# Decode attention: reading a whole segment's page numbers ahead of its first load

## The reference

```
past_kv = cache_kv_latent[l][page_table].reshape(DB, past_len, KV_LORA)
past_pe = cache_k_rope[l][page_table].reshape(DB, past_len, QK_ROPE)
o_lat = mla_attend(q_lat, q_pe, ((past_kv, past_pe, past_mask), (c_kv, k_pe, self_mask)))
```

## Time and profile before

| what | value |
|---|---|
| time, median of 3 runs | 1570.84 us (1568.0, 1570.84, 1571.12) |
| the profiled execution's own time | 1564.77 us |
| its span | 1563.0 us |
| PE busy | 1468.2 us, 94% of the span |
| PE busy in the slices of the decode attention | 7 to 8 tenths |
| granted TensorE clock, mean | 0.975 of full speed |
| page loads | 128 of 128 KB and 128 of 32 KB, from SP and POOL |

### The profile page before, as it was taken

The page is one execution under the profiler, slowest core; times in us unless marked ns, Lnnn a source line. Parts: engine busy times, 40 slices in busy tenths (PEclk is TensorE's granted clock), DMA queues, the critical chain, the costliest instruction groups (busy, mean ns, idle before and its releaser), DMA issues. The chain is left out here.

```text
span 1563.0 us, 26508 instructions
## 1 busy us (share of the span) xinstructions
PE 1468.2 (94%) x9613; PEld 1249.5 (80%) x9613; DVE 805.1 (52%) x1462; ACT 590.6 (38%) x1263; POOL 400.7 (26%) x524
## 2 busy tenths in 40 slices
PE   5999999899989988878999999999999999999997
PEld 5997877676867866556888989999999999787786
DVE  4512200054456644333149565566556665698877
ACT  5420111123433333222045444454444544544454
POOL 3136530040030005524001543444444442000000
PEclk9999999998989999987999999999999999999999
DMA  6421223433330005553231323332233324855764
GB/s 231 157 94 50 101 104 112 140 113 112 104 107 5 1 7 166 163 163 96 83 124 57 108 72 105 107 91 81 82 107 107 107 75 167 282 196 160 250 219 172
DMA packets 143247, 186.79 MB, mean 120 GB/s; under 512 B 22899, under 2 KB 89700, under 8 KB 142966
## 3 DMA queue, kind: packets, MB, share of 16 engines
q1 hardware_dynamic: 137294, 174.37, 34.6%
q0 software_dynamic: 4800, 9.84, 2.3%
q10 hardware_dynamic: 1056, 1.31, 0.3%
HBM read 149.25 MB, written 36.19 MB: 119 GB/s over the span
## 5 line engine op out<-in xcount | busy, mean ns | idle before, releaser
L2916 PE MATMUL p_ff<-s_xh,s_ff_rhi 128*128 128x266 f32 x608 | 176.7, 291 | 13.0 <-DVE s_ff_u L2714 10.2
L2916 PE MATMUL p_ff<-s_ff_th,s_ff_rhi 128*128 128x266 f32 x640 | 184.6, 288 | 0.8 <-ACT s_ff_u L2501 0.5
L2918 PE MATMUL p_ff<-s_ff_tl,s_ff_rhi 128*128 128x266 f32 x640 | 183.2, 286 | 0.0
L2919 PE MATMUL p_ff<-s_ff_th,s_ff_rlo 128*128 128x266 f32 x640 | 183.2, 286 | 0.0
L2918 PE MATMUL p_ff<-s_xl,s_ff_rhi 128*128 128x266 f32 x608 | 175.0, 288 | 0.0
L2919 PE MATMUL p_ff<-s_xh,s_ff_rlo 128*128 128x266 f32 x608 | 175.0, 288 | 0.0
L118 PE MATMUL p_ip<-s_ip_hi,s_xh 128*128 128x512 f32 (+2 forms) x400 | 149.1, 373 | 1.4 <-DVE s_xl L216 1.4
L120 PE MATMUL p_ip<-s_ip_hi,s_xl 128*128 128x512 f32 (+2 forms) x400 | 148.3, 371 | 0.0
L119 PE MATMUL p_ip<-s_ip_lo,s_xh 128*128 128x512 f32 (+2 forms) x400 | 148.1, 370 | 0.0
L2916 PEld LDWEIGHTS p_ff<-s_xh,s_ff_rhi 128*128 128x128 f32 x608 | 116.0, 191 | 23.5 <-DVE s_ff_rlo L2688 11.7
L3021 PE MATMUL p_ff<-s_fd_wh,s_fd_ah 128*128 128x512 f32 x308 | 121.7, 395 | 5.5 <-DVE s_fd_wl L2795 4.3
(11 more groups left out here) (312 smaller groups left out, 3139.4 us busy)
## 6 DMA issues: line engine op xcount, KB each, us to landing
s_ff_raw<-in_w_up SPq DMA_DIRECT2D x44, 512.0 KB, 4.6
s_fd_lanes<-in_w_down SPq DMA_DIRECT2D x77, 256.0 KB, 3.6
s_fd_lanes<-a_rows SPq DMA_DIRECT2D x66, 256.0 KB, 3.4
a_rows<-s_ff_cv SPq DMA_DIRECT2D x22, 512.0 KB, 3.0
s_ff_scr<-in_w_down SPq DMA_DIRECT2D x11, 1024.0 KB, 6.1
s_ip_raw<-in_w_in SPq DMA_DIRECT2D x4, 2048.0 KB, 8.9
s_pages<-in_cache_kv_latent SPq DMA_DIRECT2D x60, 128.0 KB, 2.1
s_pages<-in_cache_kv_latent POOLq DMA_DIRECT2D x52, 128.0 KB, 2.4
```

The lines of the kernel that those rows point to most:

```text
L2916: pe.matmul(out, rhi[:, s, ks_], hi_cols(k), start=first and k == 0, stop=False, skip_group_check=True)
L2918: pe.matmul(out, rhi[:, s, ks_], lo_cols(k), start=False, stop=False, skip_group_check=True)
L2919: mm = pe.matmul(out, rlo[:, s, ks_], hi_cols(k), start=False, stop=last and k == 3, skip_group_check=True)
```

## The change

Before, each issuer read a page's number just ahead of the load that uses it, behind the wait for that page's buffer. Now, for segments 1, 2 and 3, it reads all numbers of the segment into registers first, 17 on SP and 15 on POOL, and then goes through waits and loads. `AHEAD` (8, all pages of a segment) says for how many pages at a time. Segment 0 is read as before.

```diff
+AHEAD = SEGP
...
+    def number(self, eng, s, p, b):
+        g, half = divmod(s, HALVES)
+        at = (GB * g + b) * NPAGE + half * SEGP + p
+        return eng.value_load(self.page_sb[0:1, at:at + 1], min_val=0, max_val=self.x["cache_kv_latent"].shape[1] - 1)
+
+    def numbers_sync(self, sp, s, ps):
+        return {p: [self.number(sp, s, p, b) for b in range(self.share(p))] for p in ps}
...
-    def load(self, eng, s, p, batches, issuer):
+    def load(self, eng, s, p, batches, issuer, numbers=None):
...
-        for b in batches:
-            at = (GB * g + b) * NPAGE + half * SEGP + p
-            page = eng.value_load(self.page_sb[0:1, at:at + 1], min_val=0, max_val=latents.shape[1] - 1)
+        for i, b in enumerate(batches):
+            page = numbers[i] if numbers else self.number(eng, s, p, b)
...
                 for s in range(1, SEGS):
-                    for p in range(SEGP):
-                        if s >= 2:
-                            sp.wait_ge(S["out_done"], (s - 2) * SEGP + p + 1)
-                        pages.load_sync(sp, s, p)
+                    for p0 in range(0, SEGP, AHEAD):
+                        numbers = pages.numbers_sync(sp, s, range(p0, p0 + AHEAD))
+                        for p in range(p0, p0 + AHEAD):
+                            if s >= 2:
+                                sp.wait_ge(S["out_done"], (s - 2) * SEGP + p + 1)
+                            pages.load_sync(sp, s, p, numbers[p])
                     if has_own(s - 1):
                         sp.wait_ge(S["out_done"], s * SEGP)
                         own_values(s // HALVES)
```

More of the change, by code:

```diff
@@ L1377, in load_table, with numbers_pool @@
                      ).then_inc(self.table, 16)
-    def load(self, eng, s, p, batches, issuer):
+    def number(self, eng, s, p, b):
[4 more added lines that the diff above has]
+        return {p: [self.number(sp, s, p, b) for b in range(self.share(p))] for p in ps}
+    def numbers_pool(self, pool, s, ps):
+        return {p: [self.number(pool, s, p, b) for b in range(self.share(p), GB)] for p in ps}
+    def load(self, eng, s, p, batches, issuer, numbers=None):
         latents, ropes = self.x["cache_kv_latent"], self.x["cache_k_rope"]
-        g, half = divmod(s, HALVES)
-        for b in batches:
-            at = (GB * g + b) * NPAGE + half * SEGP + p
-            page = eng.value_load(self.page_sb[0:1, at:at + 1], min_val=0, max_val=latents.shape[1] - 1)
+        for i, b in enumerate(batches):
+            page = numbers[i] if numbers else self.number(eng, s, p, b)
             for cache, dst in ((latents, self.kv), (ropes, self.pe)):
@@ L1393, in share, with load_sync, load_pool @@
         return 3 if p % 8 == 3 else 2
[L1395 to L1399, removed]
+    def load_sync(self, sp, s, p, numbers=None):
+        self.load(sp, s, p, range(self.share(p)), "sync", numbers)
+    def load_pool(self, pool, s, p, numbers=None):
+        self.load(pool, s, p, range(self.share(p), GB), "pool", numbers)
     def wait_unit(self, eng, s, u):
@@ L1531, in _ @@
                 for s in range(1, SEGS):
[L1532 to L1535, removed]
+                    for p0 in range(0, SEGP, AHEAD):
+                        numbers = pages.numbers_pool(pool, s, range(p0, p0 + AHEAD))
+                        for p in range(p0, p0 + AHEAD):
+                            if s >= 2:
+                                pool.wait_ge(S["out_done"], (s - 2) * SEGP + p + 1)
+                            pages.load_pool(pool, s, p, numbers[p])
             @block.scalar
```

## The result

The changed kernel takes 1574.3 us (median of 16 runs, 1570.76 to 1579.26), the kernel before 1567.55 on the same chips (16 runs, 1562.68 to 1571.49). The ratio is 1.0042, with a 95% interval of 1.003 to 1.0055: slower by 6.6 us, 4.7 to 8.6.

A forecast was written before the change was run, and what follows sets the result against it. PE's waits for cached pages in decode attention, 8.4 us, were taken as the bound; 0 in segments 1 and 2 plus 4.1 in segment 3 on 1570.84 gave 1574.9 us, range 1570.5 to 1579.5.

The forecast's parts named there:

- A read in a row costs 0.58: On SP, each page-number read was taken at 0.58 us even in a row, so 17 reads take 9.9 us.
- the rival that would have made the change a gain: Reads in a row are cheap, 0.17 us each on SP: 9.4 us faster in all, 1561.4 us; 12 in 100.
- The estimate by the unrolling in the Trainium skill: Four register loads unrolled to spread a floor of about 600 ns: SP's 17 reads an estimated 3 us instead of 9.9.
- Bare loads at 1.04 on SP, 1.17 on POOL: Page loads without a read follow each other after 1.04 us on SP and 1.17 on POOL, instead of 1.62 and 1.74.
- Segment 1 costs nothing: SP's first load goes out at 601.5 instead of 592.26; any delay is taken up by PE's wait at segment 2's start.
- Two stalls like the one named: Two SP DMA stalls, like one of 1.02 us instead of 0.33, would make segment 1's second unit 0.9 us late.
- Segment 2 comes out even, -0.5 to +1.5: SP's first load goes out 6.1 us late, but PE's waits at the first two units only change places: 0.
- Segment 3 costs 4.1: Nothing covers SP's reads behind the own values' load: first unit 6.5 us late, two later waits go, 4.1 us slower.
- The rival on the transfers: Transfers set the pace of bare loads, say 1.3 us each: 5.5 to 7 us later, 1577 us; 10 in 100.
- The end of the phase: Decode attention behind the page loads' last unit: no gain or loss was put into the sum.

The follow-up runs named there:

- e3: Changed kernel, but SP reads segment 3's numbers ahead of the wait for the own values; 1561.59 us, ratio 0.9971 to the kernel before.
- e2: Changed kernel, but SP reads each number ahead of its load again, so only POOL reads ahead; 1567.6 us, ratio 0.9992 to the kernel before.
- e1: Changed kernel, but POOL reads each number ahead of its load again, so only SP reads ahead; 1572.18 us, ratio 1.0036 to the kernel before.
- e8: Kernel before, but SP reads segment 2's numbers in the preceding phase and segment 3's ahead of the own values' wait; 1559.94 us, ratio 0.9961 to the kernel before.
- e7: Changed kernel, but SP reads segment 3's numbers twice; 1584.57 us, ratio 1.0113 to the kernel before.

## Why the prediction was right, and where its sizes were off

The time, 1574.3, lies beside the predicted 1574.9, but it was measured against 1567.55: the change cost 6.6 us (4.7 to 8.6) where I forecast 4.1. That the two times lie so close is partly luck: I had started from 1570.84, the median of three runs. The mechanism was right; the term that was too small is the landing. Point by point:

- *A read in a row costs 0.58.* 0.55: right. That reads in a row would share their cost, the rival that would have made the change a gain, fell. The estimate by the unrolling in the Trainium skill (DMA: Bandwidth & Descriptors, "Latency and other measured facts"), 0.18 a read, fell with it: here the measurement decides. Nor does the Trainium skill's floor of about 600 ns hold for the load itself, which took 0.27 us; the 0.58 that I set beside it was the whole read with its checks.
- *Bare loads at 1.04 on SP, 1.17 on POOL.* 1.03 and 1.17 (632.00 to 633.17 in POOL's timeline): right.
- *Segment 1 costs nothing.* PE waited 1.64 us at (1,1), as that unit landed 4.2 us behind its last issue where I took 2.1. The wait at (2,0), where SP's issue decides, took it up. Right in the sum. (Two stalls like the one named would make (1,1) 0.7 late, not 0.9.)
- *Segment 2 comes out even, -0.5 to +1.5.* It did not: from the start of the phase to the own values' load it took 77.84 us against 75.57, 2.3 more. The first 48 transposes were slower too, 8.48 us against 7.15 (7.24 in e3, 8.21 in e2), but that can't be the reason: PE then stood 4.28 us at (2,0) for SP, which had not had to wait for a buffer since the phase began. SP's first load of segment 2 went out 6.1 late, as forecast. Then its four loads of (2,0) took 4.1 us to issue where I took 3.6, and the last landed 3.5 us behind its issue of 639.56 where I took 2.1. The way from (2,0) to (2,2) was 13.3 us where I took 12.8; in it PE waited 0.75 for DVE to empty the transposes' banks. The wait at (2,1) went.
- *Segment 3 costs 4.1.* From the own values' load to (3,2) it took 30.73 us against 24.84 (695.98 - 665.25): 5.9. The first load went out 9.1 later, forecast 9.3. The mis-sized terms: the landing of (3,0), 3.4 us behind its last issue of 679.64 where I took 2.3, the issue of its four loads, 4.0 us where I took 3.6, and the way from (3,0) to (3,2), 12.9 us where I took 12.5. I had read the landings off rows at a DMA share of 0.70 and kept them for the quicker loads. The rival on the transfers named this effect with the wrong price: but for single stalls pace was not lost, the landings got longer.
- *The end of the phase.* I had it unchanged. From (3,3) to the output projection it took 28.6 us before and 26.3 after, so 2.3 came back there. The last weighing took 6.10 us and the product behind it 3.31 at a granted clock of 0.61 (701 to 717 us), and 5.37 and 1.96 at 0.76 (714 to 728 us). In e1 to e8 this end took 26.1 to 26.8 us, but 28.6 in e2. What sets it was not tried, and whether the 2.3 us belong to the change or to the one execution traced of each kernel is not shown. Without them the trace's loss would be 8.2 us, twice the forecast.

So 2.3 + 5.9 - 2.3 = 5.9 us, by which the phase grew. e1 shows that it is SP's part, e3 that segment 3's share is the order against the own values' wait, and e7 that the reads there lie bare on the path. That the long landing costs 1.7 us at (3,0) is shown by e7; for the 1.4 us at (2,0) no run sets POOL's transfers aside.

## What to carry to other kernels

Work that is moved ahead of a wait is free only up to the time in which the engine waited: count it against that idle time, issuer by issuer and wait by wait, and look whether another wait stands between the two places. Here POOL had 8 us of idle time ahead of segment 2 for 8.3 us of reads, SP 3.2 us for 9.3 and, behind the own values' wait, none; the same reads put where SP was idle gave -0.7% instead of +0.4%. A gain for one of two issuers shows only when the other isn't the last. And where loads go out faster, look at how long each takes to land as well as at when it is issued.

## What the runs showed that I had not expected

- With both issuers at full pace the DMA engines were 0.94 to 0.95 busy, 283 to 291 GB/s, and SP kept its 1.03 us a load but for single stalls; the landings grew, from 2.1 to 3.4 us, and fell to 1.9 where SP was alone (e7).
- A DMA issue of SP stalled now and then at the full pace too, but no oftener: 1.0 us and more three times in the 51 loads of segments 1 to 3, before and after.
